# Coefficient spans between the U blocks, 16-bit one-hots with three weight parts, and earlier loads in a hybrid encoder with PEER

## What is computed

```python
x = x + merged @ w_out          # merged = sigmoid(ga) * (oa @ w_br_a) + sigmoid(gb) * (ob @ w_br_b)
x = x + peer(rms_norm(x, g_ffn), w_pq, sub_keys, u_emb, v_emb)
```

```python
a = einsum('ckd,cd->ck', u_emb[ec], hc)                   # ec: the experts, gc: their softmax weights
coef = gelu(a) * gc
out = einsum('ck,ckd->cd', coef, v_emb[ec])
```

## Time and profile before

| what | value |
|---|---|
| runs | 4104.26 us median, 4102.55 to 4108.33 (3 runs) |
| profiled execution | 4106.35 us, its span 4104.4 us, mean granted PE clock 0.911 |
| busy share of the span | PE 86%, DVE 76%, ACT 35%, POOL 19% |
| DMA | 1099.74 MB, mean 268 GB/s |
| chain that ended last | PE 59%, DVE 16%, issue 10%, DMA 7%, POOL 3%, ACT 3% |

### The profile page before, as it was taken

The page is one execution under the profiler, slowest core; times in us unless marked ns, Lnnn a source line. Parts: engine busy times, 40 slices in busy tenths (PEclk is TensorE's granted clock), DMA queues, the critical chain, the costliest instruction groups (busy, mean ns, idle before and its releaser), DMA issues.

```text
span 4104.4 us, 59985 instructions
## 1 busy us (share of the span) xinstructions
PE 3545.6 (86%) x22044; PEld 3216.7 (78%) x22046; DVE 3100.8 (76%) x3905; ACT 1421.2 (35%) x1936; POOL 774.5 (19%) x772
## 2 busy tenths in 40 slices
PE   7997998861998469878988768999998999999997
PEld 6876997761776359867988768998878999998786
DVE  4654444458898778877799997778888788887887
ACT  4544433431444124323322102334442233333443
POOL 0000000000212532221121222222220032232221
PEclk9999998985999679989999757999996799999999
DMA  6651655541998779988887657989994399998997
GB/s 192 192 172 51 180 158 164 179 128 63 348 339 304 284 284 364 341 312 315 301 291 291 227 190 273 339 329 353 353 364 171 123 349 353 350 350 325 354 355 304
DMA packets 288246, 1099.74 MB, mean 268 GB/s; under 512 B 24832, under 2 KB 25216, under 8 KB 219008
## 3 DMA queue, kind: packets, MB, share of 16 engines
q1 hardware_dynamic: 208640, 528.55, 37.7%
q0 software_dynamic: 73728, 536.90, 34.3%
q10 hardware_dynamic: 5760, 32.80, 2.1%
HBM read 1087.67 MB, written 10.49 MB: 268 GB/s over the span
## 4 chain that ended last, share of the span: by engine, by line
PE 59%; DVE 16%; issue 10%; DMA 7%; POOL 3%; ACT 3%; DVEq 0%; ACTq 0%; PEldq 0%; POOLq 0%; PEld 0%; SPq 0%
PE ps L1090 17%; PE ps L1142 14%; PE ps L1314 10%; PE ps L1086 9%; DMA w<-v_emb 5%; PE ps L1125 4%; DVE rows L638 4%; PE ps L1287 3%; POOL rows L305 3%; DVE w_lo L655 2%; DVE w_lo L622 1%; ACT w_hi L327 1%; DMA w<-w_out 1%; DVE acc L642 1%; DVE pick L977 1%
## 5 line engine op out<-in xcount | busy, mean ns | idle before, releaser
L622 DVE TENSOR_TENSOR w_lo<-w,w_hi 128x1024 fp32r<-128x1024 f32 x752 | 918.9, 1224 | 609.4 <-ACT w_hi L327 580.5
L327 ACT ACTIVATE w_hi<-w 128x1024 fp32r<-128x1024 f32 x752 | 795.8, 1060 | 1243.4 <-PE ps L1090 381.0
L303 POOL TENSOR_TENSOR tick<-iota 128x1 f32<-128x1 f32 x256 | 142.0, 555 | 3176.0 <-DVE acc L642 1135.1
L642 DVE SCALAR_TENSOR_TENSOR acc<-rows,stage_d,acc 128x2048 f32<-128x2048 f32 x256 | 600.6, 2346 | 2.1 <-DVE stage_d L633 1.2
L638 DVE CUSTOM_DVE_ANT_0 rows<-rows,h 128x2048 f32<-128x2048 f32 x256 | 584.6, 2286 | 7.0 <-DMA rows<-u_emb,stage_i 3.7
L655 DVE TENSOR_TENSOR w_lo<-ps,w_hi 128x1024 fp32r<-128x1024 f32 x256 | 312.6, 1222 | 145.7 <-ACT w_hi L394 133.8
L394 ACT ACTIVATE w_hi<-ps 128x1024 fp32r<-128x1024 f32 x256 | 262.8, 1027 | 438.5 <-PE ps L1125 438.5
L1142 PE MATMUL ps<-ht_hi,w_lo 128*128 128x256 f32 x2048 | 295.6, 288 | 39.7 <-DVE w_lo L655 39.4
L305 POOL DMA_INDIRECT rows<-v_emb,stage_i x256 | 318.2, 1243 | 57.3 <-issue 39.1
L305 POOL DMA_INDIRECT rows<-u_emb,stage_i x256 | 314.0, 1227 | 57.8 <-issue 40.0
L1086 PE MATMUL ps<-w_lo,ht_hi 128*128 128x512 f32 x1024 | 280.1, 396 | 41.6 <-DVE w_lo L622 41.4
(11 more groups left out here) (180 smaller groups left out, 5145.3 us busy)
## 6 DMA issues: line engine op xcount, KB each, us to landing
w<-w_in SPq DMA_DIRECT2D x320, 512.0 KB, 3.9
w<-u_emb SPq DMA_DIRECT2D x256, 512.0 KB, 6.6
w<-v_emb SPq DMA_DIRECT2D x256, 512.0 KB, 6.7
w<-w_out SPq DMA_DIRECT2D x64, 512.0 KB, 4.7
w<-w_pq SPq DMA_DIRECT2D x64, 512.0 KB, 5.0
w<-w_br_b SPq DMA_DIRECT2D x32, 512.0 KB, 4.7
xin<-x ACTq DMA_DIRECT2D x4, 2048.0 KB, 8.8
w<-w_br_a SPq DMA_DIRECT2D x16, 512.0 KB, 4.0
```

Of the source, the lines that this page charges most:

```text
L327: act.activation(w_hi[:, j % 2, :, :], w[:, j % RING, :, :], ACT.Copy).then_inc(hi_ready, 1)
L622: dve.tensor_tensor(w_lo[:, j % 2, :, :], w[:, j % RING, :, :], w_hi[:, j % 2, :, :].bitcast(F32), ALU.subtract).then_inc(lo_ready, 1)
L642: dve.scalar_tensor_tensor(acc[:, t, :], row, stage_d[:, j:j + 1], acc[:, t, :], ALU.mult, ALU.add).then_inc(used, 1)
```

## The change

- Spans have no stretch of their own any more. In half 0 a span follows each of the 32 U blocks, in half 1 every second of the 64. Between two blocks PE runs the span's matmuls in PSUM banks 6 and 7. Since a span now finds some U blocks done and others not, coefs is filled from both sides: where the gelu came first, DVE multiplies the span onto it (weigh_span), where the span came first, ACT copies it (spread_out), and DVE later multiplies the gelu onto it (weigh_block).
- The one-hots are bfloat16, with the token as the innermost index (8 tokens, so a token's elements lie 16 bytes apart). The weight is split into three 16-bit parts instead of two of float32, so that a span has 24 matmuls instead of 16. Number tables and keys (iota8, sel_key) are kept in 16 bits.
- The turns stand elsewhere: U_TURNS (16, 112), V_TURNS 64; their sum is the same. acc is loaded beside block 22 of half 0.
- x is loaded in two halves ahead of everything else, SP's first weight loads wait for it, gvec and ident come next. PE waits for ident alone; DVE waits for the other constants after its first pair of qkv tiles.
- Branch: tiles alternate between two sets of PSUM banks, and a tile's gating, sum and split stand between the slabs of the next tile.
- Out: the wait for x is put ahead of the first residual, that for gvec ahead of the norm. pq: the two issues stand behind ACT's splits 1 and 3.

The diff, cut to its core:

```diff
-G_TURNS, U_TURNS, V_TURNS = TOK // SPAN, (48, 96), 56
+G_TURNS, U_TURNS, V_TURNS = 32, (16, 112), 64
+SPANS = TOK // SPAN
+PARTS = 3
...
-    match1 = at("match1", R_SPLIT + 16384, [2, SPAN, HB], BF16)
+    pick1 = (at("pick1_even", R_SPLIT + 16384, [PARTS, HB, SPAN], BF16), pick1_odd)
+    pick2 = at("pick2", R_RAW + 65536, [2, NKEYS, SPAN], BF16)
+    match1 = at("match1", R_RAW + 71680, [HB, SPAN], BF16)
+    sel_w = at("sel_w", R_RAW + 72704, [TOK], F32)
...
+    def coefs_before(h, b):
+        return b if h == 0 else b // 2
+    def blocks_before(h, i):
+        return EARLY + i + 1 if h == 0 else 2 * i + 2
+    def span_after(h, b):
+        return b if h == 0 else b // 2 if b % 2 else None
+    def made(h, b):
+        return b if h == 0 else SPANS - 1 + b - 1
...
+            sp.wait_ge(x_first, 16)
+            sp.wait_ge(x_in, 16)
...
-            act.dma_start(xin[:, :, :], xs[0]).then_inc(x_in, 16)
-            for dst, src in ((ident[:, :], ident_c), (rope_a[:, :, :, :], rope_a_c), (rope_b[:, :, :, :, :], rope_b_c),
+            act.dma_start(xin[:, 0, :], x[0, 0:P, :]).then_inc(x_first, 16)
+            act.dma_start(xin[:, 1, :], x[0, P:2 * P, :]).then_inc(x_in, 16)
+            act.dma_start(gvec[:, :], g_mix_b).then_inc(g_in, 16)
+            act.dma_start(ident[:, :], ident_c).then_inc(ident_in, 16)
+            for dst, src in ((rope_a[:, :, :, :], rope_a_c), (rope_b[:, :, :, :, :], rope_b_c),
                              (gain[:, :, :], gains), (mask[:, :, :], mask_c), (iota[:, :], iota_c)):
                 act.dma_start(dst, src).then_inc(consts_in, 16)
-                if src is ident_c:
-                    act.dma_start(gvec[:, :], g_mix_b).then_inc(g_in, 16)
...
+            def u_with_coefs(h, b0, beside):
+                g0 = table_g0[h][0] + 2 * b0
+                def activate(b):
+                    act.wait_ge(slab_done, g0 + 2 * b + 4)
+                    n_ = SPAN * coefs_before(h, b)
+                    if n_:
+                        if coefs_before(h, max(b - 2, 0)):
+                            act.wait_ge(c_made, made(h, b - 2))
+                        act.activation(ge[:, b % 2, 0:n_], ps[:, 4 + b % 2, 0:n_], ACT.Gelu)
+                    act.activation(coefs[:, b0 + b, n_:], ps[:, 4 + b % 2, n_:TOK], ACT.Gelu).then_inc(a_free, 1)
+                def spread_out(i):
+                    k0 = blocks_before(h, i)
+                    act.wait_ge(picks_free, SPANS * h + i + 3)
+                    act.activation(coefs[:, k0:, SPAN * i:SPAN * (i + 1)],
+                                   ps[:, 6 + i % 2, :].rearrange("p (m k) -> p k m", m=SPAN)[:, k0:, :], ACT.Copy).then_inc(spread, 1)
+                for b in range(HB - b0):
+                    turned_hi(g0 + 2 * b, 0, 2 * (HB * h + b0 + b))
+                    if b:
+                        activate(b - 1)
+                    turned_hi(g0 + 2 * b + 1, 1, 2 * (HB * h + b0 + b) + 1)
+                    if b and span_after(h, b - 1) is not None:
+                        spread_out(span_after(h, b - 1))
+                    beside(b)
+                activate(HB - b0 - 1)
...
                 for ct in range(4):
                     for k in range(BR_SLABS):
                         gg = ph["branch"]["g0"] + BR_SLABS * ct + k
                         split_hi(gg, gg % RING)
-                    act.wait_ge(merged, 4 * r + ct + 1)
-                    act.activation(ht_hi[:, 4 * ct:4 * ct + 4, :], m1[:, :, :], ACT.Copy).then_inc(merged_hi, 1)
+                        if k == 3 and ct:
+                            merged_out(ct - 1)
+                merged_out(3)
...
-                act.dma_start(yr, x1[:, :, :]).then_inc(y_out, 16)
-                act.dma_start(skn[:, :, :], sub_keys.rearrange("c n d -> n c d")).then_inc(sk_in, 16)
                 for i in range(2 * ph["pq"]["pairs"] * SPC):
                     split_hi(ph["pq"]["g0"] + i, i % RING)
+                    if i == 1:
+                        act.dma_start(yr, x1[:, :, :]).then_inc(y_out, 16)
+                    if i == 3:
+                        act.dma_start(skn[:, :, :], sub_keys.rearrange("c n d -> n c d")).then_inc(sk_in, 16)
...
+                def dots_out(b):
+                    if h == 0 and b == 22:
+                        act.wait_ge(dots_done, 1)
+                        act.dma_start(acc[:, :, :], yr[0]).then_inc(x1_back, 16)
+                        act.activation(coef[:, :, :], dots[:, :, :], ACT.Gelu).then_inc(gelu_done, 1)
+                u_with_coefs(h, 0 if h else EARLY, dots_out)
...
-            dve.wait_ge(consts_in, 96)
...
+                dve.wait_ge(consts_in, 80)
...
                 for ct in range(4):
                     for k in range(BR_SLABS):
                         gg = ph["branch"]["g0"] + BR_SLABS * ct + k
                         split_lo(gg, gg % RING)
                         turns(r, 0 if k % 3 == 2 else 1)
...
+                        if k == 1 and ct:
+                            gated(ct - 1, 1)
+                        if k == 2 and ct:
+                            summed(ct - 1)
+                        if k == 4:
+                            if ct:
+                                merged_lo(ct - 1)
+                                dve.wait_ge(m1_free, 4 * r + ct)
+                            gated(ct, 0)
+                gated(3, 1)
+                summed(3)
+                merged_lo(3)
...
-                dve.wait_ge(xres_in, 16 * (r + 1))
-                dve.wait_ge(g2_in, 16 * (r + 1))
                 def residual(ct):
+                    if ct == 0:
+                        dve.wait_ge(xres_in, 16 * (r + 1))
...
+                dve.wait_ge(g2_in, 16 * (r + 1))
...
+                    span = slice(SPAN * i, SPAN * (i + 1))
+                    dve.wait_ge(picks_free, SPANS * h + i + 1)
+                    dve.tensor_tensor(match1[:, :, :], iota8[:, HB * h:HB * (h + 1), :],
+                                      sel_key[:, 0, span].unsqueeze(1).to_broadcast([P, HB, SPAN]),
+                                      ALU.is_equal).then_inc(matched, 1)
+                    dve.tensor_tensor(pick2[:, i % 2, :, :], iota8[:, :, :],
+                                      sel_key[:, 1, span].unsqueeze(1).to_broadcast([P, NKEYS, SPAN]), ALU.is_equal)
+                    dve.wait_ge(matched, SPANS * h + i + 1)
+                    dve.tensor_tensor(pick1[i % 2][:, :, :, :], match1[:, :, :].unsqueeze(1).to_broadcast([P, PARTS, HB, SPAN]),
+                                      weight_part[:, :, span].unsqueeze(2).to_broadcast([P, PARTS, HB, SPAN]),
...
+                def weigh_span(i):
+                    k1 = blocks_before(h, i)
+                    if k1 < HB:
+                        dve.wait_ge(spread, 2 + (SPANS - 1) * h + i + 1)
...
+                    dve.wait_ge(a_free, 2 + HB * h + k1)
+                    cs = coefs[:, 0:k1, SPAN * i:SPAN * (i + 1)]
+                    dve.tensor_tensor(cs, cs, ps[:, 6 + i % 2, :].rearrange("p (m k) -> p k m", m=SPAN)[:, 0:k1, :],
+                                      ALU.mult).then_inc(weighed, 1)
...
+                def weigh_block(b):
+                    n_ = SPAN * coefs_before(h, b)
+                    if n_:
+                        dve.wait_ge(a_free, b + (HB * h + b0 + 3))
+                        dve.wait_ge(spread, 2 + (SPANS - 1) * h + coefs_before(h, b))
+                        cb = coefs[:, b0 + b, 0:n_]
+                        dve.tensor_tensor(cb, cb, ge[:, b % 2, 0:n_], ALU.mult).then_inc(c_made, 1)
...
+                for b in range(HB - b0):
+                    j = 2 * b
+                    split_turned(table_g0[h][0] + 2 * b0 + j, j)
+                    late_turns((due(max(b - 1, 0)) + due(b)) // 2 if h or b != 24 else due(b - 1))
+                    split_turned(table_g0[h][0] + 2 * b0 + j + 1, j + 1)
+                    if span_after(h, b) is not None:
+                        picks(span_after(h, b))
+                    if b:
+                        weigh_block(b - 1)
+                        if span_after(h, b - 1) is not None:
+                            weigh_span(span_after(h, b - 1))
+                    if h == 0 and b == 24:
+                        dve.wait_ge(gelu_done, 1)
+                        own.after(dve, dve.tensor_tensor(coef[:, :, :], coef[:, :, :], gsel[0][:, :, :], ALU.mult))
+                        dve.wait_ge(x1_back, 16)
+                    late_turns(due(b))
+                    if h == 0 and b == 20:
+                        assert took[0] == G_TURNS
+                        dve.wait_ge(copied, GROUPS + 1)
+                        dve.drain().then_inc(dots_done, 1)
+                weigh_block(HB - b0 - 1)
+                weigh_span(SPANS - 1)
                 leave(dve, "dve"); n += 1
                 enter(dve, "dve", n)
@@ -1063,10 +1150,10 @@
...
             pe.sem_inc(acc_free, 2)
-            for sem in (picks_free, spread, weighed, a_free, c_made):
...
+            def u_with_coefs(h, b0):
```

(81 more changed lines are left out.)

172 lines of the change are left out of this document (72 added, 100 removed).

## The result

The kernel after takes 3982.64 us (median of 4 runs, 3977.25 to 3985.43) against 4105.85 us of the kernel before beside it: a ratio of 0.9699, 95% interval 0.9682 to 0.9716, some 123 us less. The forecast was 193 us less, 3911 us; the direction was right and the time lies inside the range, close to its high end. The profiled execution took 3984.77 us, its span 3983.0.

The account below looks back on a forecast made before the run. U blocks were taken as bound by TensorE, with spans wasting DMA time at half clock. From 4106.35 us, -7 -21 -5 -8 -7 -3 -118 -40 +16 = -193 gave 3913, less 2.1: 3911 us; range 3850 to 3990.

Parts of the forecast that it names:

- Half 0: Spans and U blocks of half 0: 320 us forecast against 438.0, a term of -118 us.
- The high end: Upper limit of the whole kernel's range: 3990 us, with dearer spans, V turns in line and no gain in request 1's front.
- V: V stretches: 64 gather turns instead of 56 in each, taken as +8 us each, +16 us in all.
- The span's price: TensorE's 24 matmuls per span: 2.0 us, between 1.3 from weight loads and 2.6 from transposes; farthest 5.1 us.
- Rival (1): Span matmuls: strided operand reads are slow, 5.1 us per span, 191 us back, kernel at 4102 us; chance 0.09.
- Rival (2): U blocks: granted clock falls behind spans; half clock half the time costs 424 us, kernel at 4335; chance 0.09.
- Half 1: Spans and U blocks of half 1: 561 us forecast against 600.9, a term of -40 us; 17.0 us per block pair.
- rival (3): Picks in the U blocks: VectorE becomes the bound with picks at 3.4 us, kernel at 3954 us; chance 0.10.
- Rival (4): DMA takes the gain back: V pays 24 instead of 8 twice, request 1's front gives nothing; 3955 us; chance 0.08.
- Branch: Branch stage: with two pairs of PSUM banks TensorE need not wait; -21 us in request 0, -5 in request 1.
- Out with the head of pq: Later waits for x and gvec: -8 us in request 0, -7 in request 1; two moved pq issues: -1.6 each.
- The start: Kernel start: x loaded first and VectorE's first norm step no longer waiting for the last constant, together -7 us.

## Why the prediction was right, and where it was wrong

**Right in direction, for the reason given in half 0 alone.** There the old spans took a stretch of 178.1 us at half clock, at VectorE's pace and with the DMA at 0.48 (the 3% of the prediction is half 1's), and the load of acc stood in the open behind them (a window of the kernel before, and a line of its chain):

```profile
2313.40:2491.50 178.10, 115.91 (x512) 111.61 (x512) 175.52 (x206) 12.26 (x32) 50.24 (x48) 0.50 0.48 179
2491.92 12.57 DMA acc<-y
```

Between the U blocks the same 32 spans cost 32 x 2.95 us and 6 us of slow pieces, 100 us, and the load of acc is covered. Half 0 brings 94.5 us and the front 59.1; the other three stretches give 32 back. Half 0 also has 32 gather turns fewer than before (48 instead of 80). No run moves the spans with the turns left in place or with the 32-bit one-hots, so what each of these brings is not shown.

**That the time lies in the range is partly luck.** The high end had room for spans at 2.6 us (35 us) and for V and the out stage (42 us). The spans and the slow pieces alone cost 61 + 30 us more than forecast, and V 7; the front gave 8 back, and the rest of the two U sums 18.

**The span's price was the step that failed.** The prediction wrote: "I take the middle of the two nearest, 2.0 us." It was 2.95. Both nearest rows, the transpose and the weight loads, read their operands side by side, and the moving operand's steps cost most of the difference; the upper end from those rows, 2.6, did not hold either. 64 x 0.95 = 61 us. Had the operands been in rows, 2.0 would have been too much: 0.72 was below the lower end of 1.3.

**Rival (1) was half true.** Its mechanism is there, 2.95 us for reads in steps against 0.72, but it took the far end of 5.1, which is 32-bit operands at half clock. A third of the way from 2.0 to 5.1 us was gone (0.95 of 3.1 us): the kernel was held back, not brought level with before.

**Rival (2) was true on a small scale.** I treated the clock as all or nothing and held against it that a span is 2 us among 7.5 or 15 us of dots. At 2.0 us that was right, as the run with two parts shows; at 2.95 the granted clock fell behind 15 of 32 spans in half 1, 15 x 1.57 = 24 us, and 4 times in half 0, 6 us, where the rival asked for 193. So one mis-sized term carried a second loss with it.

**Half 1, point by point.** Forecast 561, measured 610. The spans add 32 x 0.95 = 30 and the falls 24; some 5 us less went into fill and end. The wait for y<-total was put at 9.7 and is 9.65. Before, it took 115 us from the stage's start to its first U blocks (3122.6 to 3238), nearly all spans at half clock, the wait in their shadow; now spans cost 32 x 2.95, falls 24 and the open wait 10: 128. That is why interleaving brought nothing there. A pair of blocks took 17.9 us without a slow piece and 19.5 with one, not the 17.0 named as a sign of being right.

**Half 0.** Forecast 320, measured 343.5: 30 from the spans, 6 from the falls, less about 13 that I had put in for VectorE's last eight blocks and for preparation and fill. The picks took 2.05 us, between my 1.7 and 2.5, and never held TensorE up, so rival (3) falls. By the Trainium skill, "VectorE: DVE Perf Modes", the perf-mode tier table, tensor_tensor on 16-bit operands in SBUF goes at twice the rate of 32-bit ones. The trace agrees in the main: the 1024-element pick went from 1.23 us to 0.68, 1.8 times.

**V.** +8 each was forecast; +9.8 and +13.1 was measured, and the run with 56 turns gives 11.5 back in each. Rival (4) asked for 24 and falls. The second stretch, 394.0 us, passes the 390 that was named as a sign of being wrong, but with the DMA at 0.91 and not at 1.00.

**The front.** -59.1 against -51. Branch: -21.9 and -6.1 (forecast -21 and -5). Out with the head of pq: request 0 took 108.5 instead of 118.1 us from out to pq, -9.6 as summed (-8 and -1.6); request 1 112.4 instead of 124.0, -11.6 against -8.6. The start: VectorE's first norm step came at 11.12 instead of 20.13, -9 against -7, though only 4.4 us of it were left at the first branch matmul; the run with the branch alone, whose start is unchanged, reached that matmul 8.7 us later than before did, so this part of the sum is no better than that. The rest, some 5 us between pq of request 0 and the branch of request 1, I had not summed. Two slips in the working decided nothing: for the branch, three and six steps of 1.22 us are 11.0 us and not 12.2, and spans at 2.6 us add 64 x 0.6 = 38 us to the high end and not 35.

## What to carry to other kernels

When an operand's layout is turned round for one engine, price it on every engine that reads it. Here 16-bit elements 16 bytes apart halved VectorE's picks and made TensorE's small matmuls 4.1 times dearer, most of it through the moving operand. A bound taken from rows whose operands lie side by side is no bound for operands that don't. And a slack resource is slack only for the present bottleneck: 16 turns were free before the spans became short, and cost 35 us after.

## What the hardware showed that I had not expected

- The moving operand's steps weigh more than those of the weights, though it has 64 columns and they have 128: putting the moving one in rows takes 1.46 us off a span (2.95 to 1.49), putting the weights in rows 0.15 us (2.95 to 2.80), and 0.77 us only once the moving one is in rows (1.49 to 0.72).
- A 16-bit tensor_tensor of 1536 elements took 0.95 us with all innermost steps at one element, 1.75 with one input repeated along the innermost axis, and 7.2 with its output written 128 bytes apart.
- The granted clock fell for some 3 us behind spans of 2.80 to 2.95 us in one piece, and the same work in pieces of 1.13 us left it at 0.99. It also fell behind two spans of 0.87 and 0.91 us ahead of which TensorE had waited 1.8 us for a pick.
